# Streaming the gate products of a hybrid block in halves of 256 tokens

## The reference

```
h = rmsnorm(x, mix_pre_g);  proj = h @ w_in
a_in, b_in, gates = split(proj, [2048, 3072])          # 2048 | 1024 | 4096 columns
a = silu(layernorm(causal_conv31(a_val * sigmoid(a_gate))));   y_a = a @ w_a_out
b = (trailing means of b_in over 2/4/8/16 tokens) - b_in, mapped by pool_w, scaled;  y_b = b @ w_b_out
merged = sigmoid(gates_a) * y_a + sigmoid(gates_b) * y_b
x = x + rmsnorm(merged @ w_o)
x = x + rmsnorm((gelu(u_gate) * u_val) @ w_down)       # u = causal_conv3(rmsnorm(x) @ w_up), 2 x 5632 columns
x = x + rmsnorm((p @ w_ple) * sigmoid(x @ w_ple_gate))
```

## Time and profile before

| | |
|---|---|
| median of the timed runs | 2664.44 us (2663.29 to 2665.49) |
| profiled execution, its span | 2665.0 us |
| instructions in the profile | 31629 |
| PE matmuls, busy | 11714, 2637.8 us |
| PE weight loads, busy | 11714, 2184.9 us |
| VectorE busy | 1348.2 us |
| ScalarE busy | 806.5 us |
| DMA | 277.26 MB, mean 104 GB/s |
| TensorE clock, mean granted | 0.996 |

### The profile page before, as it was taken

How to read it: one execution, slowest core, us unless ns; L and a number is a source line. 1 busy time by engine, 2 the same in 40 slices (tenths; PEclk the granted TensorE clock), 3 DMA queues, 4 the chain that set the end, 5 groups by cost and what they waited for, 6 DMA issues and landing times.

```text
span 2665.0 us, 31629 instructions
## 1 busy us (share of the span) xinstructions
PE 2637.8 (99%) x11714; PEld 2184.9 (82%) x11714; DVE 1348.2 (51%) x1693; ACT 806.5 (30%) x972; POOL 13.5 (1%) x34
## 2 busy tenths in 40 slices
PE   8999999999999999999999999999999999999998
PEld 7888888888888877888888888888888888888886
DVE  6888766643334237444445444444454444446534
ACT  5222322342223234332323232222222222224423
POOL 0000000000000001000000000000000000000000
PEclk9999999999999999999999999999999999999999
DMA  5333333333334324333333333333333333343332
GB/s 163 103 95 100 98 95 99 91 115 99 95 95 161 100 79 150 95 95 98 100 95 95 97 101 96 95 96 101 96 95 96 101 97 95 96 172 103 104 103 103
DMA packets 384842, 277.26 MB, mean 104 GB/s; under 512 B 8116, under 2 KB 337500, under 8 KB 383708
## 3 DMA queue, kind: packets, MB, share of 16 engines
q1 hardware_dynamic: 380512, 259.03, 32.3%
q0 software_dynamic: 1296, 12.06, 1.2%
q10 hardware_dynamic: 2924, 4.54, 0.5%
HBM read 267.21 MB, written 8.39 MB: 103 GB/s over the span
## 4 chain that ended last, share of the span: by engine, by line
PE 98%; DVE 1%; ACT 1%; DMA 0%; issue 0%; DVEq 0%; ACTq 0%
PE ps L400 22%; PE ps L402 22%; PE ps L401 22%; PE ps L466 10%; PE ps L468 10%; PE ps L467 10%; PE ps L428 1%; ACT squares_out L654 0%; DVE e_buf L977 0%; DVE diag L959 0%; DMA x_nat<-in_x 0%; PE ps L478 0%; ACT xg_hi L659 0%; DVE x L977 0%; DVE w_lo L944 0%
## 5 line engine op out<-in xcount | busy, mean ns | idle before, releaser
L944 DVE TENSOR_TENSOR w_lo<-w_raw,w_hi 128x1024 fp32r<-128x1024 f32 x478 | 585.0, 1225 | 1186.1 <-ACT w_hi L639 1185.6
L400 PE MATMUL ps<-xg_hi,w_hi 128*128 128x512 f32 x2304 | 899.6, 390 | 1.6 <-DVE w_lo L944 1.6
L402 PE MATMUL ps<-xg_hi,w_lo 128*128 128x512 f32 x2304 | 898.1, 390 | 0.0
L401 PE MATMUL ps<-xg_lo,w_hi 128*128 128x512 f32 x2304 | 898.0, 390 | 0.0
L639 ACT ACTIVATE w_hi<-w_raw 128x1024 fp32r<-128x1024 f32 x478 | 506.0, 1060 | 1129.7 <-PE ps L402 599.2
L400 PEld LDWEIGHTS ps<-xg_hi,w_hi 128*128 128x128 f32 x2304 | 433.6, 188 | 92.5 <-issue 1.8
L402 PEld LDWEIGHTS ps<-xg_hi,w_lo 128*128 128x128 f32 x2304 | 433.5, 188 | 90.2
L401 PEld LDWEIGHTS ps<-xg_lo,w_hi 128*128 128x128 f32 x2304 | 433.6, 188 | 89.8
L466 PE MATMUL ps<-w_hi,g_hi 128*128 128x512 f32 x704 | 273.9, 389 | 0.0
L468 PE MATMUL ps<-w_lo,g_hi 128*128 128x512 f32 x704 | 273.9, 389 | 0.0
L467 PE MATMUL ps<-w_hi,g_lo 128*128 128x512 f32 x704 | 273.9, 389 | 0.0
(11 more groups left out here) (165 smaller groups left out, 1830.3 us busy)
## 6 DMA issues: line engine op xcount, KB each, us to landing
w_raw<-in_w_up SPq DMA_DIRECT2D x176, 512.0 KB, 3.9
w_raw<-in_w_in SPq DMA_DIRECT2D x112, 512.0 KB, 3.7
w_raw<-in_w_down SPq DMA_DIRECT2D x88, 512.0 KB, 3.7
w_raw<-in_w_o SPq DMA_DIRECT2D x32, 512.0 KB, 3.7
w_raw<-in_w_ple_gate SPq DMA_DIRECT2D x32, 512.0 KB, 3.7
w_raw<-in_w_b_out SPq DMA_DIRECT2D x16, 512.0 KB, 3.9
w_raw<-in_w_a_out SPq DMA_DIRECT2D x16, 512.0 KB, 4.0
x_nat<-in_x SPq DMA_DIRECT2D x4, 1024.0 KB, 9.6
```

The lines of the kernel that those rows point to most:

```text
L400: pe.matmul(o, w_hi[:, s, cols], hi, start=start, stop=False)
L401: pe.matmul(o, w_hi[:, s, cols], lo, start=False, stop=False)
L402: return pe.matmul(o, w_lo[:, s, cols], hi, start=False, stop=stop)
L944: dve.tensor_tensor(w_lo[:, s], w_raw[:, u.slot(RAW)], as_f32(w_hi[:, s]), ALU.subtract).then_inc(lo_ready, 1)
```

## The change

Two new functions take the place of `tile` in two places. `pair_tile`, for the eight pooling tiles, leaves the two products with `w_hi` at 512 tokens and makes the one with `w_lo` as two matmuls of 256 tokens, one behind the other, with the same weights. `half_tile`, for the twelve gate tiles of the loop L556, walks over all 16 chunks for the first 256 tokens and then over all 16 again for the other 256, three products each; it waits for the weights in the first walk and releases each unit in the second. Branch tiles, the other gate tiles and all other engines' programs stay as they are.

```diff
+            def pair_tile(u, t):
+
+                bank_free(t, 4)
+                for k in range(DC):
+                    if k % 8 == 0:
+                        pe.wait_ge(lo_ready, (u + (k // 8 + 1)).value())
+                    o, s, cols = ps[:, t.slot(4)], (u + k // 8).slot(SLOTS), slice(k % 8 * P, (k % 8 + 1) * P)
+                    pe.matmul(o, w_hi[:, s, cols], xg_hi[:, k], start=k == 0, stop=False)
+                    pe.matmul(o, w_hi[:, s, cols], xg_lo[:, k], start=False, stop=False)
+                    for h in range(2):
+                        tok = slice(h * HALF, (h + 1) * HALF)
+                        last = pe.matmul(o[:, tok], w_lo[:, s, cols], xg_hi[:, k, tok], start=False, stop=h == 1 and k == DC - 1)
+                    if k % 8 == 7:
+                        last.then_inc(units_done, 1)
+
+            def half_tile(u, t):
+
+                bank_free(t, 4)
+                for h in range(2):
+                    o, tok = ps[:, t.slot(4), h * HALF:(h + 1) * HALF], slice(h * HALF, (h + 1) * HALF)
+                    for k in range(DC):
+                        if h == 0 and k % 8 == 0:
+                            pe.wait_ge(lo_ready, (u + (k // 8 + 1)).value())
+                        s, cols = (u + k // 8).slot(SLOTS), slice(k % 8 * P, (k % 8 + 1) * P)
+                        pe.matmul(o, w_hi[:, s, cols], xg_hi[:, k, tok], start=k == 0, stop=False)
+                        pe.matmul(o, w_hi[:, s, cols], xg_lo[:, k, tok], start=False, stop=False)
+                        last = pe.matmul(o, w_lo[:, s, cols], xg_hi[:, k, tok], start=False, stop=k == DC - 1)
+                        if h == 1 and k % 8 == 7:
+                            last.then_inc(units_done, 1)
...
             with pe.Fori(0, 2) as i:
                 for j in range(4):
-                    tile(At(U_B + 2 * j, i, 8), At(T_B + j, i, 4), xg_hi, xg_lo)
+                    pair_tile(At(U_B + 2 * j, i, 8), At(T_B + j, i, 4))
...
-                if gate:
+                if gate and halves:
+                    half_tile(u, t)
+                elif gate:
                     tile(u, t, xg_hi, xg_lo, between=within_gate)
...
                 for j in range(4):
-                    branch(At(U_M2 + 3 * j, i, 12), At(T_M2 + 2 * j, i, 8), a_hi, a_lo)
+                    branch(At(U_M2 + 3 * j, i, 12), At(T_M2 + 2 * j, i, 8), a_hi, a_lo, halves=True)
```

More of the change, by code:

```diff
@@ L402, in products @@
                 return pe.matmul(o, w_lo[:, s, cols], hi, start=False, stop=stop)
+            HALF = TOK // 2
+            def pair_tile(u, t):
[24 more added lines that the diff above has]
+                            last.then_inc(units_done, 1)
             def chunk_products(o, u, k, hi, lo, chunks):
@@ L520, in _, with branch @@
                     last.then_inc(units_done, 1)
-            def branch(u, t, hi, lo, arrives=None, ahead_of_branch=None, within_gate=None, gate=True):
-                if gate:
+            def branch(u, t, hi, lo, arrives=None, ahead_of_branch=None, within_gate=None, gate=True, halves=False):
+                if gate and halves:
+                    half_tile(u, t)
+                elif gate:
                     tile(u, t, xg_hi, xg_lo, between=within_gate)
```

## The result

The changed kernel takes 2673.80 us (median of 6 runs, 2671.84 to 2676.87) against 2664.71 for the kernel before in its six (2662.98 to 2665.49): a ratio of 1.0037, 95% interval 1.0025 to 1.0050. It is slower, by 9.1 us of the medians. That is rival B's time to a tenth (2673.8), inside the stated range, and not the forecast of no measurable change.

What follows compares the result with a forecast made beforehand. PE's matmul count times its step was taken as the bound. Splits (0.9 us) and unsettled steps (1.0) made 1.9 us on the 2665.0 span, 0.6 above the median 2664.44: from the median 2666.3 us, range 2661 to 2676.

Steps and rivals of the forecast that it cites:

- rival B: Split gate and pooling tiles: 13.3 ns come once per matmul, step 120.0 ns, 9.4 us more, 2673.8 us; chance 0.26.
- the change is paid on PE alone and in full: Pooling and L556 loops: PE is busy throughout, so every added nanosecond counts; weight supply and other engines cost nothing.
- 704 splits, each with a load of its own: Pooling tiles add 128 matmuls, gate tiles 576, each loading its weights: 12418 matmuls in all.
- The load as a floor at 111 ns: Split tiles: a weight load takes 111 ns, so the step at 256 columns is at least that.
- the leftover: In each 512-column fp32r step of 226.7 ns, the 13.3 ns over the 213.3 for columns at 2.4 GHz.
- 704 x 1.3 = 0.9 us: Cost of all splits in pooling and gate tiles, at 228.0 - 226.7 = 1.3 ns each.
- The two rows I argued from: L540's full-width pass, 1.3 ns over its columns, and fp32r at 1.2 GHz, nothing over; taken against a fixed cost.
- A: Split tiles: the 13.3 ns scale with columns, step near 114 ns, 2666.3 us; the forecast itself, chance 0.55.
- The isolated product at 817.34: Last product before the output projection: no load beside it, still 0.39 us; counted little against the load as cause.
- The disturbance term (1.0 us): Pooling tiles: wide products beside halves stay unsettled, 256 x 4.4 ns = 1.1 us; bounds 0 and 4.2, taken 1.0.
- the sign that I had set: Split tiles: the forecast is wrong if s, the step at 256 columns, is outside 111 to 117 ns.

Runs made afterwards that it cites:

- the quarters: The changed kernel's twelve gate tiles streamed in quarters of 128 tokens, the pooling tiles left as before; executed once, 2793.13 us.
- halves apart: The changed kernel with its pooling products ordered full, half, full, half, gate tiles as before; executed once, 2667.80 us.

## Why the prediction was right or wrong

- That the change is paid on PE alone and in full: right. No wait of PE appeared in the loops, VectorE and ScalarE did the same work, and the sum of the turns, 10.1 us, lies in the interval of the 9.1 measured.
- 704 splits, each with a load of its own: right (12418 of both).
- The load as a floor at 111 ns: right; the quarters show it at 112. By an estimate from these steps it is the bound below some 235 columns (111 less 13.3, times 2.4).
- **The step that failed** is the one that divided the leftover: "A fixed cost per matmul would have shown in both". I took 1.3 ns fixed and 12.0 proportional; measured are 13.3 fixed and nothing proportional (120.0, 173.3 and 226.7 at 256, 384 and 512 columns). The term "704 x 1.3 = 0.9 us" is 704 x 13.3 = 9.4. The two rows I argued from are true and of other conditions: plain float streams at half the rate, and at 1.2 GHz the columns take twice as long. That a cost is hidden at half the rate says nothing on whether it scales with columns at the full rate: bfloat16's 2.5 ns, fixed by its two widths, are gone at 1.2 GHz just so (427 ns a step). No row of the trace had fp32r at a second width and full clock, and the answer hung on just that; 0.55 for A was too much on an argument by analogy, and 0.26 for B too little.
- The isolated product at 817.34 as a hint that the load isn't the cause: not contradicted; a load of half the columns saved nothing. Whether a matmul without any load before it would pay the 13.3 wasn't tried.
- The disturbance term (1.0 us): of the right kind. Over 13.3 ns a split the pooling tiles cost 3.4 x 128 = 0.4 us more, and a turn of the other loop took 2.64 us where 192 x 13.3 ns are 2.56, 0.2 us in three turns: 0.6 in all. But its parts were wrong. The wide pooling products carry 6.5 ns each where 4.4 was my bound, and the halves beside them, at 115.2, are nearer to my 114.0 than to 120. The step of 120.0 is that of the gate tiles, where 96 matmuls of one width follow each other, and 576 of the 704 splits are there.
- The range held because it reached past B. That is luck and no merit of the mechanism: by the sign that I had set (s outside 111 to 117 ns) the forecast was wrong, as s is 120.

## What to carry to other kernels

Where TensorE's step is the bound, find its constant and its slope before splitting or merging streams: steps of one width can't give both, and constants differ by operand type (13.3 ns for fp32r, 2.5 for bfloat16 in one piece). Stream fp32r as wide as a bank allows (512 columns here), keep one type and one width in a run of matmuls, and if three bfloat16 products are precise enough, weigh them against three fp32r ones: here they took 4.5% less. What they do to the error is to be measured for each use.

## What the runs showed of the hardware that I had not expected

- The fixed part of a matmul shows at the full clock alone: at 1.2 GHz 512 columns step at 0.427 us in fp32r and in bfloat16 alike, nothing over.
- A bfloat16 view that takes two bytes of every four steps at 225 ns for 512 columns and 113 for 256: nearly all of its leftover goes with the columns; bfloat16 in one piece has 215.8 and 109.2.
- At a change from fp32r to bfloat16 the load starts late (PEld idle 0.27 us before it); two changes in three matmuls cost 21 ns a chunk.
- Widths mixed within a chunk cost beside the fixed part: 3.4 ns a split for halves in pairs, 13.3 for halves apart.
